# Maxima spread by broadcast transfers, four reordered waits and a first load on another queue in a one-core decoder layer

## The reference

```python
x = x + 0.5 * swiglu(rmsnorm(x, ffn1_norm), ...)        # D_FF = 2816
h = rmsnorm(x, mix_norm)
proj = h @ w_in                                         # q,k | v | o | i,f gates | pool channels
qk = silu(causal_dwconv(proj[q,k], conv_w, conv_b))     # width 4
hm = mlstm_chunkwise(q, k, v, i_pre, f_pre)             # 4 heads of 128, causal, stabilised by running maxima
hm = sigmoid(o) * rmsnorm_per_head(hm) * mh_norm
hp = multiscale_pool(proj[pool], pool_w, pool_scale)    # causal means over 2, 4, 8, 16 minus self
x = x + concat(hm, hp) @ w_out
x = x + 0.5 * swiglu(rmsnorm(x, ffn2_norm), ...)
return rmsnorm(x, final_norm)
```

## Time and profile before

| What | Value |
|---|---|
| Median of 3 runs | 905.66 us (905.58 to 906.29) |
| The profiled execution | 905.16 us |
| Its span, first to last instruction | 903.4 us, 15625 instructions |
| PE busy | 892.4 us (99%) |
| PE weight loads busy | 806.4 us (89%) |
| DVE busy | 680.7 us (75%) |
| ACT busy | 457.0 us (51%) |
| POOL busy | 43.8 us (5%) |
| DMA | 91.73 MB, mean 102 GB/s |
| Mean granted TensorE clock | 0.997 of full speed |

### The profile page before, as it was taken

How to read it: one execution, slowest core, us unless ns; L and a number is a source line. 1 busy time by engine, 2 the same in 40 slices (tenths; PEclk the granted TensorE clock), 3 DMA queues, 4 the chain that set the end, 5 groups by cost and what they waited for, 6 DMA issues and landing times.

```text
span 903.4 us, 15625 instructions
## 1 busy us (share of the span) xinstructions
PE 892.4 (99%) x5590; PEld 806.4 (89%) x5590; DVE 680.7 (75%) x1174; ACT 457.0 (51%) x754; POOL 43.8 (5%) x63
## 2 busy tenths in 40 slices
PE   9999999999999999999999999999999999999996
PEld 7899999999888888888888788999999999888886
DVE  7999999998643434677887779899999998634334
ACT  7665666565432323444862465566656665423221
POOL 0000000000000000001535100000000000000000
PEclk9999999999999999999999999999999999999998
DMA  6232333332432333222212232233333332433312
GB/s 244 94 117 95 104 104 115 94 104 89 146 116 96 114 99 111 70 93 70 71 48 79 87 115 71 94 105 104 113 96 102 107 105 83 140 115 98 112 47 94
DMA packets 38996, 91.73 MB, mean 102 GB/s; under 512 B 4288, under 2 KB 6464, under 8 KB 38960
## 3 DMA queue, kind: packets, MB, share of 16 engines
q1 hardware_dynamic: 38640, 90.72, 30.5%
q0 software_dynamic: 176, 0.46, 0.2%
q10 hardware_dynamic: 144, 0.08, 0.0%
HBM read 89.14 MB, written 2.10 MB: 101 GB/s over the span
## 4 chain that ended last, share of the span: by engine, by line
PE 95%; DVE 3%; ACT 1%; issue 0%; DVEq 0%; ACTq 0%
PE ps L366 16%; PE ps L367 16%; PE ps L368 16%; PE ps L471 14%; PE ps L473 14%; PE ps L472 14%; PE ps L417 1%; PE ps L396 1%; PE ps L399 1%; PE ps L402 1%; PE ps L782 0%; DVE w_lo L1252 0%; PE ps L643 0%; DVE xg_lo L1258 0%; PE ps L635 0%
## 5 line engine op out<-in xcount | busy, mean ns | idle before, releaser
L1252 DVE TENSOR_TENSOR w_lo<-raw,w_hi 128x1024 fp32r<-128x1024 f32 x83 | 102.8, 1240 | 120.2 <-ACT w_hi L806 114.6
L366 PE MATMUL ps<-act_hi,w_hi 128*128 128x512 f32 (+1 forms) x470 | 178.9, 381 | 0.2 <-DVE act_lo L1730 0.2
L368 PE MATMUL ps<-act_hi,w_lo 128*128 128x512 f32 (+1 forms) x470 | 178.2, 379 | 0.0
L367 PE MATMUL ps<-act_lo,w_hi 128*128 128x512 f32 (+1 forms) x470 | 178.2, 379 | 0.0
L471 PE MATMUL ps<-xg_hi,w_hi 128*128 128x256 f32 x608 | 174.0, 286 | 0.0
L473 PE MATMUL ps<-xg_hi,w_lo 128*128 128x256 f32 x608 | 172.2, 283 | 0.0
L472 PE MATMUL ps<-xg_lo,w_hi 128*128 128x256 f32 x608 | 171.9, 283 | 0.0
L806 ACT ACTIVATE w_hi<-raw 128x1024 fp32r<-128x1024 f32 x75 | 79.1, 1056 | 152.8 <-PE ps L368 149.1
L471 PE MATMUL ps<-xe_hi,w_hi 128*128 128x256 f32 x456 | 128.0, 281 | 0.6 <-ACT work L900 0.6
L473 PE MATMUL ps<-xe_hi,w_lo 128*128 128x256 f32 x456 | 127.2, 279 | 0.0
L472 PE MATMUL ps<-xe_lo,w_hi 128*128 128x256 f32 x456 | 127.2, 279 | 0.0
(11 more groups left out here) (220 smaller groups left out, 1401.7 us busy)
## 6 DMA issues: line engine op xcount, KB each, us to landing
raw<-weights SPq DMA_DIRECT2D x85, 512.0 KB, 3.3
raw<-weights SPq DMA_DIRECT2D x152, 256.0 KB, 2.6
x<-x_t SPq DMA_DIRECT2D x8, 256.0 KB, 6.0
first<-weights SPq DMA_DIRECT2D x8, 256.0 KB, 6.0
out<-x SPq DMA_DIRECT2D x6, 256.0 KB, 2.3
out<-x SPq DMA_DIRECT2D x4, 128.0 KB, 2.1
arena<-pool_w POOLq DMA_DIRECT2D x1, 256.0 KB, 2.9
vec<-vecs ACTq DMA_DIRECT2D x1, 74.0 KB, 2.6
```

What stands on the lines that cost most here:

```text
L366: pe.matmul(acc, hi, m_hi, start=first, stop=False)
L367: pe.matmul(acc, hi, m_lo, start=False, stop=False)
L368: return pe.matmul(acc, lo, m_hi, start=False, stop=last)
L1252: dve.tensor_tensor(w_lo[:, k % SLOTS], raw[:, k % RAWS], f32(w_hi[:, k % SLOTS]), ALU.subtract).then_inc(lo_made, 1)
```

## The change

It has five parts. The diff below leaves out declarations of semaphores and the deleted helper bodies' neighbours.

1. At the start the first block of weights is issued by ScalarE, as its first instruction, ahead of the scalars. SP issues the rest in the old order.
2. The maxima no longer go through PE. VectorE writes the negated maxima once, in float32 (`neg_m`, four rows of the tile `sums`). SP stores them to a tensor in HBM and waits for that, then loads one row for each head into `r_all[h % 2]` with the same row read for all 128 partitions. `spread`, `copy_r`, the selector and the low part of the maxima are gone, and so are PE's waits for the copies. SP's loads of the units MIX+15 to MIX+19 stand between these transfers and their waits.
3. In VectorE's first Strassen iteration `act_low` of the last plain block comes after `sum_1` and `sum_3`, not before the iteration.
4. In `out_blocks` of stages 1 and 2, for the last tile of x, the split of x comes ahead of the split of the weights.
5. In the output projection half of block 2 is computed ahead of the last parts of blocks 0 and 1.

```diff
@@ SP, start
             for k in range(KD):
                 if k == 0:
                     sp.dma_start(x[:, k], x_t[k * P:(k + 1) * P]).then_inc(x_in[k], 16)
-                sp.dma_start(first4[:, k], weights[k // 2, :, (k % 2) * T:(k % 2 + 1) * T]).then_inc(first_in[k], 16)
-                if k > 0:
+                else:
+                    sp.dma_start(first4[:, k], weights[k // 2, :, (k % 2) * T:(k % 2 + 1) * T]).then_inc(first_in[k], 16)
                     sp.dma_start(x[:, k], x_t[k * P:(k + 1) * P]).then_inc(x_in[k], 16)
@@ ScalarE, start
+            act.dma_start(first4[:, 0], weights[0, :, 0:T]).then_inc(first_in[0], 16)
             act.dma_start(vec[:], vecs).then_inc(vec_in, 16)
@@ SP, units of the mixer
-            units(DN1 + RAWS, DN2)
+            def spread_row(h):
+                sp.dma_start(r_all[h % 2], neg_rows[h:h + 1].partition_broadcast(P)).then_inc(r_in[h % 2], 16)
+            def unit(n):
+                sp.wait_ge(lo_made, n - RAWS + 1)
+                load(n, n)
+            units(DN1 + RAWS, MIX + 15)
+            sp.wait_ge(neg_made, 1)
+            sp.dma_start(neg_rows, neg_m).then_inc(neg_out, 16)
+            sp.wait_ge(neg_out, 16)
+            spread_row(0)
+            unit(MIX + 15)
+            unit(MIX + 16)
+            sp.wait_ge(qk_made, 2 * HEADS)
+            spread_row(1)
+            sp.wait_ge(e_made, 1)
+            spread_row(2)
+            unit(MIX + 17)
+            unit(MIX + 18)
+            sp.wait_ge(e_made, 2)
+            spread_row(3)
+            units(MIX + 19, DN2)
@@ PE, mixer
-                def spread(h):
...
-                    for part in neg_m:
-                        mm = pe.matmul(bank, sel[:, h * P:(h + 1) * P], part, start=part is neg_m[0],
-                                       stop=part is neg_m[1])
-                    mm.then_inc(r_rep, 1)
@@ scores(0)
                         pe.wait_ge(cols_made, 2)
-                        pe.wait_ge(r_copied, 1)
@@ head_rep(h)
                     pe.wait_ge(hcol_step, HSTEPS * (h + 1))
-                    pe.wait_ge(r_copied, min(h + 3, HEADS))
+                    if h >= 1:
+                        pe.wait_ge(hm_made, h)
@@ PE, output projection
                 part(1, (5,))
+                pe.wait_ge(lo_made, WO_UNIT + 3)
+                part(2, (0, 1, 2, 3), first=True)
                 part(0, (4,), last=True)
                 part(1, (4,), last=True)
-                for d in range(2, KD):
+                part(2, (7, 6, 5, 4), last=True)
+                for d in range(3, KD):
@@ ScalarE, mixer
-                def copy_r(h):
-                    act.wait_ge(r_rep, h + 1)
-                    if h >= 2:
-                        act.wait_ge(r_diag_made, h - 1)
-                    act.activation(r_all[h % 2], ps[:, r_bank[h]], ACT.Copy).then_inc(r_copied, 1)
@@ weights_of(h); the same on GpSimd
-                    act.wait_ge(r_copied, h + 1)
+                    act.wait_ge(r_in[h % 2], 16 * (h // 2 + 1))
@@ VectorE, Strassen iteration
                         sum_1(s + 1)
                         sum_3(s + 1)
+                        if head:
+                            act_low(PLAIN[p] - 1)
                         sum_2(s + 1)
@@ before the iterations
                 plain_product(PLAIN[p] - 1)
-                act_low(PLAIN[p] - 1)
                 iteration(0, 0, head=True)
@@ VectorE, out_blocks
+                    last_x_first = stage < 3 and d == KD - 1
+                    if last_x_first:
+                        dve.wait_ge(x_new, KD * (stage - 1) + d + 1)
+                        split_xg(d, stage)
                     if n + SLOTS + per - 1 < N_UNITS:
                         split_lo(n + SLOTS + per - 1, n + SLOTS + per - 1)
-                    if stage < 3:
+                    if stage < 3 and not last_x_first:
                         dve.wait_ge(x_new, KD * (stage - 1) + d + 1)
                         split_xg(d, stage)
                     add_square(d, stage)
@@ VectorE, gates_second
-                    gates_then(dve.tensor_scalar(neg_m[0], M, -1.0, None, ALU.mult), 9)
-                    dve.scalar_tensor_tensor(neg_m[1], M, -1.0, f32(neg_m[0]), ALU.mult, ALU.subtract)
-                    for h in range(HEADS):
-                        dve.tensor_scalar(sel[:, h * P:(h + 1) * P], ones[R, :], ident[R, h:h + 1], None, ALU.mult)
-
+                    dve.tensor_scalar(neg_m, M, -1.0, None, ALU.mult).then_inc(neg_made, 1)
```

More of the change, by code:

```diff
@@ L103, with build_layer @@
 S_COLS = 1280
-def build_layer(nc, weights, pool_w, x_t, vecs, consts, out):
+def build_layer(nc, weights, pool_w, x_t, vecs, consts, neg_rows, out):
     ctx = ExitStack()
@@ L126, in build_layer @@
         act_lo = sb("act_lo", [P, FB, T], F32R)
-        QK, VB, SC, PO, PW, NM, SEL = 0, 8, 12, 15, 17, 18, 19
+        QK, VB, SC, PO, PW = 0, 8, 12, 15, 17
         work = sb("work", [P, 5, T])
@@ L176, in build_layer @@
         pool_sums = ((work[:, 3], work[:, 4]), (arena[:, 0], arena[:, 1]))
-        neg_m = (act_hi[0:HEADS, NM], act_lo[0:HEADS, NM])
-        sel = act_hi[0:HEADS, SEL]
+        neg_m = sums[0:HEADS, 0]
         p_hi = act_hi[:, SC:SC + 3].rearrange("p a n -> p (a n)")[:, 0:S_COLS]
@@ L184, in build_layer @@
         v_bank = (0, 7, 5, 6)
-        r_bank = (2, 7, 7, 7)
         def proj_bank(i):
@@ L226, in build_layer @@
         o_scaled, o_made = sem("o_scaled"), sem("o_made")
-        r_rep, r_copied, r_diag_made, e_made = sem("r_rep"), sem("r_copied"), sem("r_diag_made"), sem("e_made")
+        neg_out = sem("neg_out")
+        neg_made, r_diag_made, e_made = sem("neg_made"), sem("r_diag_made"), sem("e_made")
+        r_in = [sem(f"r_in{i}") for i in range(2)]
         sc_made, p_made, p_hi_made, p_split = sem("sc_made"), sem("p_made"), sem("p_hi_made"), sem("p_split")
@@ L665, in before @@
                             values(0)
-                            spread(2)
-                        if i == 2 and k == 5:
-                            spread(3)
                         if mean_of is not None and k == MEAN_AT[i]:
@@ L729, in mixer @@
                         mm.then_inc(cols_made, 1)
-                        spread(0)
                 scores(0)
@@ L736, in mixer @@
                         scores(h + 1)
-                    if h == 0:
-                        spread(1)
-                    else:
+                    if h >= 1:
                         values(h)
@@ L1065, in mixer @@
                     pending = i if n in QK_UNIT else None
-                copy_r(0)
                 finish_qk(pending)
@@ L1129, in mixer @@
                 act.wait_ge(qk_made, 2 * HEADS)
-                copy_r(1)
                 split_next()
@@ L1138, in mixer @@
                 probs_hi(1)
-                copy_r(2)
                 split_next()
@@ L1148, in mixer @@
                         probs_hi(h + 1)
-                    if h + 2 < HEADS:
-                        copy_r(h + 2)
                     split_next()
@@ L1197, in _ @@
             for h in range(HEADS):
-                pool.wait_ge(r_copied, h + 1)
+                pool.wait_ge(r_in[h % 2], 16 * (h // 2 + 1))
                 if h == 0:
@@ L1932 @@
     out = nc.dram_tensor("out", (D, T), F32, kind="ExternalOutput").ap()
-    build_layer(nc, *args, out)
+    neg_rows = nc.dram_tensor("neg_rows", (HEADS, T), F32, kind="Internal").ap()
+    build_layer(nc, *args, neg_rows, out)
     r = run_bass_kernel_spmd(nc, [arrays], core_ids=[0])
```

## The result

The change made the kernel slower, by 0.4%. Its median was 909.64 us (seven executions), that of before beside it 905.58; the ratio is 1.0041, 95% interval 1.0031 to 1.0051. Run a second time (e16) it was 908.43 against 905.43, ratio 1.0036 [1.0023, 1.0049]. Single executions over 960 us, the profiled one of e1 among them, were disturbed and count in no ratio. The prediction was 903.2, with 904.7 as its upper end. The profiled execution took 909.78 us with a span of 908.0, so 4.6 us are to be found in it against the span of 903.4 before.

The account below looks back on a forecast made before the run. The prediction took TensorE (PE) to bound the kernel, on the last-ending chain for 95% of the span. Its terms, 0 - 0.5 + 0.84 - 2.05 - 0.48 - 0.26 = -2.45, gave 903.2 us for the median, range 901.6 to 904.7.

Parts of the forecast that it names:

- Start: Kernel start: first weights issued 0.46 us earlier, scalars behind them; no net change, 0, bounds -0.2 and +0.3.
- my fourth rival: At the start PE stays longer at 1.2 GHz, each us losing half; two give 904.2; chance 0.05.
- Head of the first loop: First Strassen loop at 58 us: first sum 0.5 earlier, third sum unmoved; -0.5, between 0 and -0.7.
- Entry of the mixer: At 357 us the square sum stays behind both splits, so the mean comes later: +0.84, bounds +0.5 and +1.0.
- Mixer: Maxima's matmuls leave PE, which then runs into VectorE's and ScalarE's chain: -2.05, bounds -1.0 and -3.4.
- the first rival: Mixer's head chain not freed, heads go at VectorE's pace: mixer -1.0, sum -1.4, 904.3; chance 0.27.
- Projection: Output projection at 511.8: twelve matmuls of block 2 cover PE's wait for the last pool channel's low part: -0.48.
- Entry of the second FFN: At 551 us: split of x earlier, late square sum covered, VectorE's 0.8 idle taken up before the loop: -0.26.
- The third: Mixer's spreads run on one DMA engine, 14.7 us instead of 2.6: some +12, 917; chance 0.05.
- The second: PE gets all of the mixer's gain: mixer -3.4 and entry +0.5, giving 901.5; chance 0.13.

Follow-up runs that it names:

- e16: The change itself, unedited, run a second time: 908.43 us, 1.0036 of before.
- e1: The changed kernel with the start put back (scalars first on ScalarE's queue, first weights on SP's): 905.41 us, 1.0006 of before.
- e2: The changed kernel with VectorE's old order at the mixer's entry put back: 906.40 us, 1.0015 of before.
- e4: The changed kernel with the low part of the last plain activation back ahead of the iteration in both Strassen loops: 907.37 us, 1.0033 of before.
- e5: The kernel before with only the start changed, first weights on ScalarE's queue ahead of the scalars: 907.97 us, 1.0024 of before.
- e3: The changed kernel with VectorE's old order at the second FFN's entry put back: 907.73 us, 1.0024 of before.
- e10: The changed kernel with five unread matmuls put in PE's hole ahead of the mean's matmuls at the mixer's entry: 907.90 us, 1.0022 of before.
- e9: The same kernel as e1, run and profiled a second time: 906.90 us, 1.0011 of before.
- e13: e12 with the low part of the last plain activation moved behind two sums, as in the change: 903.81 us, 0.9982 of before.
- e15: e12 with both the edit of e13 and the edit of e14: 904.35 us, 0.9987 of before.
- e6: The kernel before with only the maxima's part changed (spread by transfers): 904.83 us, 0.9993 of before.
- e12: e8 with ScalarE's squares of head 0 ahead of the exponentials that need GpSimd: 903.90 us, 0.9982 of before.
- e7: The kernel before with the maxima's part and the output projection's order alone: 905.13 us, 0.9990 of before.
- e14: e12 with the split of x ahead of the weights at the second FFN's entry alone: 904.24 us, 0.9989 of before.
- e11: The kernel before with the first weights on ScalarE's queue, but behind the scalars: 906.09 us, 1.0010 of before.
- e8: e7 with VectorE's order at the mixer's entry made split of x, square sum, split of weights: 904.92 us, 0.9994 of before.

## Why the prediction was wrong

**Start (0, bounds -0.2 and +0.3): one of the two steps that failed most.** I saw that the scalars now stand behind 256 KB and supposed that they "land 0.9 later", with a loss of 0.2. ScalarE could round 1.92 later (5.59 for 3.67) and PE started 1.3 to 1.45 later in every profile with this start. What that costs is not one number. In e2, e4, e5 and e16 PE's matmuls were fast from the first one, where those of before are slow until 7: the delay cost 0.4 to 0.5. In after, e3 and e10 they were slow until 9.7 to 10.7: it cost 2.0 to 2.3. The longer cost is what my fourth rival said, PE longer at the low clock at half a us for each; but it was 2.7 to 3.7 us longer, where I had reckoned with two at most. In the shorter one PE was not longer at the low clock at all and lost by waiting only, which I did not have. In e5's nine runs the median is 2.5 above before. I gave the rival 0.05, on a delay that I had guessed and not bounded: the row had no transfer behind another in ScalarE's queue, and its upper bound should have been the landing of both.

The Trainium skill, "TensorE: Matmul & The Clock Gate", section "What's actually happening", says that the number of slow matmuls at a kernel's start differs from run to run of the same kernel. The traces agree: after and e16 are one kernel, and its matmuls are slow until past 10 in one and not slow at all in the other.

**Head of the first loop (-0.5): won and given back, or not won.** In after PE won 0.61 at 58 and lost 0.58 at 71.7. From 8.4 to 58.5 the five profiles with both this edit and the late start (after, e2, e3, e10, e16) win 0.60 to 0.65; the three with this edit and the old start (e9, e13, e15) win 0.12 at most, and all eight lose about 0.6 by 75. The sum's wait for its block is 0.79 in after, 0.93 in e9 and 0.88 in e13; why the start decides it is not shown. The failed sentence is that the third sum keeps its time, "since the two sums and the low part fill the same stretch": I followed PE to its next matmul, not to its next wait for VectorE. VectorE is 97% busy in such a loop (19.41 of 20 us, 580 to 600 in after), so lateness of it comes back as a stop of PE.

**Entry of the mixer (+0.84): right, but not all.** The order of the chain and its size came as written (+0.95 at the mean). What it did to the clock I left out: +1.60 by 366. In six profiles with this hole (after, e3, e4, e9, e16 and, filled, e10) the low clock followed in the five where the hole was open and not in the one where it was filled. The price of the clock is the same each time, 1.6, and larger than the hole's. These are the profiled executions; by the two heaps of e1 and e9 others may have been spared. That is the second step that failed most: the term took the hole for its whole price.

**Mixer (-2.05): the first rival, by size and by its "VectorE's pace".** By 443 PE had won 2.57 (+4.88 to +2.31). Then head 0's mean took 1.44 back, the last spread's place won 0.8 and the last values took 1.0: -0.92, in e6 -0.90. The failed sentence is that the split of the last products comes 2.0 early. Against the entry of the mixer, head 0's products came 1.10 earlier in after (435.89 for 432.11), head 1's, for which I had 1.5, only 0.85 (446.86 for 442.83), and the last split 0.91 (473.98 for 470.01); in e12, without the stop at the mean, the same three are 1.04, 0.79 and 0.93. What was lost at head 1 came from GpSimd: I had the mask additions start 1.3 earlier and last as long. They started 1.0 earlier against the rest of the chain (2.76 later than in before, where the chain was 3.8 later). But now they lay beside VectorE's split of head 0's products (439.93) as well as beside the two weight units that were there before, and took 5.38 for 3.90. The stop at head 0's mean I had overlooked, since I asked for head 1's products, not for the squares of head 0 that stand behind them in ScalarE's list. The Trainium skill, "SBUF — State Buffer", section "Who interferes with whom", says that a VectorE instruction with two inputs in SBUF contends with a GpSimd instruction that reads SBUF; the trace agrees, since the same four additions take 1.72 at 452, where VectorE runs instructions of 128x4. I had used that slowing on VectorE's side and forgotten GpSimd's.

**Projection (-0.48): right,** -0.47 in after and in e7, and kept.

**Entry of the second FFN (-0.26): right in place (-0.19), wrong in what followed.** "VectorE idles 0.8, taken up by its idle time before the loop": it had none. VectorE's squares come 4.44 later than before where PE is 3.30 later. From 552 to 660 the six profiles with both this edit and the head's (after, e2, e9, e10, e15, e16) lose 1.01 to 1.76, the four with one of them (e3, e4, e13, e14) 0.01 to 0.75, and the six with neither 0.15 to 0.74 (e6 the most). So only both together stand clear of the scatter; what one of them costs alone is not shown.

**The rivals.** The third, a broadcast on one DMA engine at 14.7 us, is refuted by the page's 3.2. The second is refuted by e6. The chances for slower (0.05) missed that two small waits can each come with the low clock, and that parts which only reorder VectorE's work borrow from a loop which VectorE fills.

**Left open.** Profiles of one kernel differ in the loops: from 75 to 340 after loses 0.03 and e16 0.68, with a stop of PE for VectorE at 90 in e16 alone; e5 loses 1.04 there, e11 nothing. They differ too in the moment of the first rise of the clock. Why the low clock follows the stop of 1.3 to 1.5 at head 0's mean in e2, e7, e8, e9 and e10, and not in after, e3, e4, e6 and e16, was not settled.

## What to carry to other kernels

A small table that everything waits for goes first in its queue; behind a transfer of 256 KB its reader started 1.92 late here. When an order is changed to close a hole, follow the instruction that was pushed back to the next wait on it, in loops above all: an engine that is 97% busy has almost no idle time to give. Price a hole in PE with the slow matmuls that may follow it, and fill it if it can't be removed.

## What was not expected of the hardware

A hole of about 1.2 us in a PE that was otherwise fully busy was followed by 1.6 us of loss at 1.2 GHz in all five profiles that have it (eight matmuls of 0.43 in after, granted clock 0.66 over 5 us). In the one profile where five matmuls whose result nobody reads filled it, it was not (clock 1.00). Mask additions of four 128x128 tiles on GpSimd took from 1.72 us, beside small instructions of VectorE, to 5.38, beside its large ones. A DMA issued 0.44 us after a 256 KB one on the same queue landed so that its reader started 1.92 later than when it was alone.
